# Moving y's products to the head of the next masked products, with lora between their halves

## The reference

```python
def rwkv7_scan(r, decay, k, v, kk, a):
    def step(S, inp):
        sa = -jnp.einsum('bhvk,bhk->bhv', S, kk_t)
        S = S * w_t[:, :, None, :] + sa[..., None] * b_t[:, :, None, :] + v_t[..., None] * k_t[:, :, None, :]
        y = jnp.einsum('bhvk,bhk->bhv', S, r_t)
        return S, y
...
mean = jnp.mean(y, axis=-1, keepdims=True)
var = jnp.mean(jnp.square(y - mean), axis=-1, keepdims=True)
y = ((y - mean) * lax.rsqrt(var + LNX_EPS)).reshape(B, T, RWKV_WIDTH) * lnx_gain + lnx_bias
```

## Time and profile before

| what | value |
|---|---|
| median of 3 runs | 1822.35 us (1821.75 to 1823.31) |
| the profiled execution | 1822.79 us, its span 1820.8 us |
| TensorE clock granted | 0.998 of full |
| busy: PE, DVE, ACT, POOL | 99%, 69%, 46%, 26% |
| chain that ended last | PE 95%, DVE 3%, ACT 1% |
| line 1404, share of that chain | 70% |

### The profile page before, as it was taken

One profiled execution on the slowest core, in us unless ns is written; L12 is line 12 of the kernel. 1 busy time (PEld: TensorE's weight loads), 2 busy tenths in 40 slices (PEclk: granted clock), 3 DMA queues, 4 the chain that ended last, 5 costly groups with the idle time before them and its releaser, 6 DMA issues.

```text
span 1820.8 us, 37389 instructions
## 1 busy us (share of the span) xinstructions
PE 1803.7 (99%) x14519; PEld 1479.8 (81%) x14519; DVE 1248.6 (69%) x2255; ACT 832.0 (46%) x1725; POOL 476.8 (26%) x1093
## 2 busy tenths in 40 slices
PE   9999999999999999999999999999999999999997
PEld 7778888888888888888888888888888788888886
DVE  5876777777767688667777777776778854345445
ACT  7544445454535355444453545353535553242335
POOL 0014233241505060142432415050606060100110
PEclk9999999999999999999999999999999999999999
DMA  8633333333333345433333333333323543466546
GB/s 302 198 92 91 92 97 86 97 92 91 98 92 99 84 108 166 114 86 92 96 87 96 92 96 95 91 100 83 106 78 107 166 138 103 130 202 202 167 126 231
DMA packets 200289, 217.09 MB, mean 119 GB/s; under 512 B 98864, under 2 KB 104112, under 8 KB 199472
## 3 DMA queue, kind: packets, MB, share of 16 engines
q1 hardware_dynamic: 190032, 197.19, 37.6%
q10 hardware_dynamic: 10080, 17.51, 3.4%
HBM read 192.61 MB, written 22.02 MB: 118 GB/s over the span
## 4 chain that ended last, share of the span: by engine, by line
PE 95%; DVE 3%; ACT 1%; issue 1%; DMA 0%; ACTq 0%; SPq 0%; DVEq 0%
PE psum L1404 70%; PE psum L1389 3%; PE psum L1679 3%; PE psum L1681 3%; PE psum L1680 3%; PE psum L1522 2%; PE psum L1462 2%; PE psum L1490 1%; PE psum L1671 1%; PE psum L1555 1%; PE psum L1635 1%; DVE w_lo L929 1%; PE psum L1642 1%; PE psum L1424 1%; PE psum L1623 1%
## 5 line engine op out<-in xcount | busy, mean ns | idle before, releaser
L1404 PE MATMUL psum<-x_hi,w_hi 128*128 128x512 f32 x1888 | 763.5, 404 | 2.5 <-DVE x_lo L938 2.2
L1404 PE MATMUL psum<-x_hi,w_lo 128*128 128x512 f32 x1888 | 738.5, 391 | 0.0
L1404 PE MATMUL psum<-x_lo,w_hi 128*128 128x512 f32 x1888 | 736.3, 390 | 0.0
L929 DVE TENSOR_TENSOR w_lo<-w_raw,w_hi 128x512 fp32r<-128x512 f32 x522 | 368.2, 707 | 393.2 <-ACT w_hi L665 362.6
L665 ACT ACTIVATE w_hi<-w_raw 128x512 fp32r<-128x512 f32 x522 | 326.1, 628 | 665.9 <-PE psum L1404 596.7
L1404 PEld LDWEIGHTS psum<-x_hi,w_hi 128*128 128x128 f32 x1888 | 355.2, 188 | 87.6 <-DVE w_lo L929 9.9
L1404 PEld LDWEIGHTS psum<-x_hi,w_lo 128*128 128x128 f32 x1888 | 354.6, 188 | 77.2
L611 POOL TENSOR_TENSOR sub_t<-sub_l,sub_io 128x60 f32<-128x60 f32 (+24 forms) x496 | 192.5, 388 | 850.1 <-DMA sub_l<-scratch_L 812.5
L1404 PEld LDWEIGHTS psum<-x_lo,w_hi 128*128 128x128 f32 x1888 | 355.7, 188 | 66.9 <-issue 0.5
L613 POOL TENSOR_TENSOR sub_io<-sub_io,sub_t 128x60 f32<-128x60 f32 (+24 forms) x496 | 207.1, 418 | 38.8
L1679 PE MATMUL psum<-w_hi,x_hi 128*128 128x512 f32 x256 | 100.3, 392 | 1.4 <-DVE w_lo L929 1.2
(11 more groups left out here) (276 smaller groups left out, 2092.8 us busy)
## 6 DMA issues: line engine op xcount, KB each, us to landing
w_raw<-in_w_in SPq DMA_DIRECT2D x348, 256.0 KB, 2.7
w_raw<-in_w_in ACTq DMA_DIRECT2D x60, 256.0 KB, 2.8
w_raw<-in_w_out SPq DMA_DIRECT2D x60, 256.0 KB, 2.7
w_raw<-in_w_rows SPq DMA_DIRECT2D x50, 256.0 KB, 2.8
stage<-in_w_rows SPq DMA_DIRECT2D x30, 256.0 KB, 2.8
sub_l<-scratch_L SPq DMA_DIRECT2D x16, 384.0 KB, 4.1
stage<-in_x_t SPq DMA_DIRECT2D x20, 256.0 KB, 4.2
stage<-scratch_MIX SPq DMA_DIRECT2D x19, 256.0 KB, 3.7
```

The lines of the kernel that those rows point to most:

```text
L929: nc.vector.tensor_tensor(w_lo[gq % SPLIT][:], w_raw[raw_of(gq)[0]][:], w_hi[gq % SPLIT][:].bitcast(F32), ALU.subtract).then_inc(w_ready, 1)
L1404: mm = nc.tensor.matmul(psum[:, bank_of(s)], wt[gq % SPLIT][:, cols], xx[:, c], start=(c == 0 and wt is w_hi and xx is x_hi), stop=(c == K ...
```

## The change

- On TensorE, y's products leave place 24. They become `outputs(i)` and stand at the head of place 25, in front of the next interval's `products(i + 1, 0)`; for intervals 6 and 15, which have no masked products there, they stand alone at the head of place 25.
- lora's products leave the place behind the masked products and stand between their two halves.
- On VectorE, the two adds of y go from place 24 to 25, behind `low` and the slices of x and in front of the masked copies. Centring goes from the end of place 24 to the end of 25. The sum of squares goes from 26 to 28, and the reciprocal and the scaling from 27 to 29.
- On ScalarE, the Square goes from 25 to 27 and the Sqrt from 27 to 29.

```diff
@@ ScalarE
-                    if at == 25:
+                    if at == 27:
                         act.wait_ge(y_centred, i + 1)
...
-                    if at == 27:
+                    if at == 29:
                         act.wait_ge(y_var, i + 1)
@@ VectorE
+                def read_y(i):
+                    dve.wait_ge(y_full, i + 1)
+                    dve.wait_ge(h_read, i + 1)
...
+                    dve.sem_inc(y_read, 1)
...
-                    if at == 24:
...
-                    if at == 26:
+                    if at == 28:
                         dve.wait_ge(y_squared, i + 1)
...
-                    if at == 27:
+                    if at == 29:
                         spread = [P, BH, HD]
                         dve.wait_ge(y_root, i + 1)
...
                     if pair:
                         slices(*pair)
                     for j, at in current(gq):
+                        if j >= 1 and at == 25:
+                            read_y(j - 1)
+                    for j, at in current(gq):
                         if j >= 1 and at == 1:
                             masked(j - 1, 0)
                             masked(j - 1, 1)
...
-                        if j >= 1 and at == 24:
+                        if j >= 1 and at == 25:
                             centre(j - 1)
@@ TensorE
+                def outputs(i):
+
+                    pe.wait_ge(gt_ready, i + 1)
...
+                    mm.then_inc(y_full, 1)
...
                 def recurrence(i, at):
                     if at == 1:
+                        if i not in (0, PAIRS - 1):
+                            outputs(i - 1)
                         products(i, 0)
+                        if i < INTERVALS - 1:
+                            lora_products(i + 1)
                         products(i, 1)
+                    if at == 25 and i in (PAIRS - 2, INTERVALS - 1):
+                        outputs(i)
```

More of the change, by code:

```diff
@@ L1206, in transition @@
                     dve.sem_inc(gt_ready, 1)
+                def read_y(i):
+                    dve.wait_ge(y_full, i + 1)
+                    dve.wait_ge(h_read, i + 1)
+                    for hh in range(2):
+                        ins = nc.vector.tensor_tensor(
+                            y[:, :, hh], psum[:, 4 + hh, 0:NB * HD].rearrange("p (b d) -> p b d", b=NB),
+                            hs[:, :, hh], ALU.add)
+                    then(ins)
+                    dve.sem_inc(y_read, 1)
                 def centre(i):
@@ L1408, in quarter, with lora_products @@
                             mm.then_inc(w_used, 1)
-                def channels(j, at):
[L1411 to L1425, removed]
+                def lora_products(j):
+                    h = j // PAIRS
+                    pe.wait_ge(up_landed[j % 2], 16 * (j // 2 + 1))
+                    pe.wait_ge(lora_ready, 2 * h + 2)
+                    pe.wait_ge(rooted, h + 1)
+                    pe.wait_ge(inv_ready, j)
+                    pe.wait_ge(bonus_read, j)
+                    if j >= 2:
+                        pe.wait_ge(mixa_ready, j - 1)
+                    if j >= 3:
+                        pe.wait_ge(yt_read, PAIRS - 1 if j == PAIRS else j - 2)
+                    for x in range(2):
+                        rows = slice(x * LORA, (x + 1) * LORA)
+                        nc.tensor.matmul(psum[:, 2 + x], lora_up[j % 2][rows, :], lora[rows, :],
+                                         start=True, stop=True).then_inc(lora_done, 1)
+                def channels(j, at):
+                    if j == 0 and at == 3:
+                        lora_products(j)
                     if at == 4 and j % PAIRS == 0:
@@ L1466, in products @@
                     mm.then_inc(a_full, 1)
+                def outputs(i):
+                    pe.wait_ge(gt_ready, i + 1)
+                    for b in range(NB):
+                        for c in range(2):
+                            for hh in range(2):
+                                rows = slice(hh * HD, (hh + 1) * HD)
+                                mm = nc.tensor.matmul(psum[vs_rows(c), 4 + hh, b * HD:(b + 1) * HD],
+                                                      gt[rows, b, c], states[rows, 2 * b + c],
+                                                      start=True, stop=True, skip_group_check=True)
+                    mm.then_inc(y_full, 1)
                 def turns(i):
@@ L1647, in recurrence @@
                         chain(i, 2 * (at - 21) + 1)
[L1648 to L1657, removed]
                     if at == 31:
```

## The result

| | before | changed kernel |
|---|---|---|
| median of 5 runs | 1822.4 us (1821.75 to 1823.44) | 1829.48 us (1827.26 to 1830.75) |
| ratio, 95% interval | | 1.0037 (1.0027 to 1.0048) |
| profiled execution | 1822.79 us | 1830.06 us |
| span, granted clock | 1820.8 us, 0.998 | 1828.1 us, 0.997 |
| busy PE, DVE, ACT, POOL | 99%, 69%, 46%, 26% | 99%, 69%, 46%, 26% |

What follows compares the result with a forecast made beforehand. PE's own list was taken as the bound. Regular heads -1.8, dead heat +0.6, break before interval 7 +0.8, interval 15 +2.0, last y +0.05: +1.7 on 1822.35 gives 1824.1 us, range 1820.8 to 1829.0.

Steps and rivals of the forecast that it cites:

- the bound: PE, busy for 99% of the span: the change gives only what it takes out of PE's own list, start to start.
- 0.76 saved at place 24: Regular interval on PE: without y the bonus follows the chain 0.13 us later instead of 0.89, so 0.76 us shorter.
- 0.63 spent at 25: Regular interval on PE: y runs 0.63 us to the first masked product, leaving a gain of 0.14 us per interval.
- lora free: PE, between the masked products' halves: lora adds nothing, it takes its 0.96 us wherever it stands.
- y_read: PE's second half of masked products waits for DVE's read of y: hidden by 0.2 us, by lora alone.
- A dead heat: Place 33: division ends so PE can go on at 231.79, PE wants its transposes at 231.78; 0.6 us over 13 intervals.
- the first rival: DVE falls behind p_norm at place 33: PE waits 0.5 us per interval, 1830 us; chance 0.24.
- interval 15: Its head: nothing gained at place 24, second half resumes 3.55 us later, old wait for masked copies goes; net +2.0 us.
- the break before interval 7: Place 24 still waits for DVE's read of a tile, y stands alone at place 25: +0.8 us, nothing back.
- ACT's fourth table load: Exp loaded again before the scores' Exp at place 31, 1.28 us, hidden by 0.3 us; as a rival 1836 us, chance 0.04.
- the late DVE: Same as the first rival: DVE late for p_norm, PE loses 13 times all beyond another 0.05 us; chance 0.24.
- The prediction's own signs of being wrong: PE's wait on the division at place 33 0.3 us or more per interval, or regular heads shorter by more than 0.3.

## Why the prediction was wrong

- **Right: the bound.** PE's own list, read from start to start, was the right ledger. 0.76 saved at place 24 (0.77), 0.63 spent at 25 (0.62), lora free (it even gave 0.02).
- **Right, with its size: y_read.** "Hidden by lora alone; without lora between, 0.7 us would be lost in each interval": 0.78 measured.
- **Wrong, the decisive step: "A dead heat … I put 0.05 us per interval".** It was 0.26 (0.20 of wait and 0.06 behind it), 3.4 us where 0.6 stood. The mechanism was right and was even the first rival; the term was mis-sized. The sum took 14 us of DVE instructions at the durations they had in the kernel before and put their end 0.01 us from the point where PE wants it. In the new order the same list is longer: from w_lo of place 28 to the end of the division the sum has 13.88 us (217.8 to 231.68), measured were 13.99 to 14.14 in 11 intervals and 14.44 to 14.45 in two. In interval 1 DVE ended 0.12 later than worked out and PE came 0.08 earlier. Errors of 0.1 us on either side have to be expected in such a sum, and they are not symmetric: coming early gives nothing, coming late costs in full, 13 times. A tie has to be priced at the spread of its terms, not at its mean. The two long intervals had a DVE pause of 0.50 us in place of the usual 0.15 (at 391.87 and 651.99), and it went through to PE (0.54 and 0.52 us at place 33); in the kernel before such a pause stood at 387.54, in slack. What makes these pauses no run here shows, but "the intervals repeat to some hundredths of a us" holds for PE's steps, not for DVE's pauses.
- **Wrong: place 36.** The prediction followed DVE's list only up to the first wait that PE has for it, and so put this term at nothing. The lateness doesn't end there; it meets the next consumer three quarters on, with 1.7 us.
- **Half right: interval 15.** The wait for y was right to 0.01 us, the release of the old wait for the masked copies too. What was missing is the clock: PE idle for 2.94 us, then 1.6 us lost at 1.2 GHz.
- **Right: the break before interval 7** (0.8 forecast, 0.9 measured), and that nothing is gained at place 24 there.
- **ACT's fourth table load** stayed hidden in the changed kernel, as worked out: ACT's work for the division ends at 229.73, where 229.8 was forecast, and DVE comes to it at 230.24. It is hidden by DVE's own lateness, though; with the sum of squares at 27, DVE waited for it. In interval 1 of the changed kernel:

```profile
226.47 1.28 ACT L753 ACT_TABLE_LOAD   x1
227.77 0.46 ACT L753 ACTIVATE score<-score,top 128x192 f32<-128x192 f32 x1
```

The Exp starts 0.02 us behind the load. The Trainium skill ("ScalarE: Activation LUTs", What ACT_TABLE_LOAD costs) puts a drain of about 1380 ns on top of each switch of table; this trace has no such time, neither behind the load nor in front of it (the w_hi before it started at 225.82 and ended at 226.45).

The range ended at 1829.0 because the late DVE was given 0.24 and its upper part left out. With the clock and place 36 missing, the sum would have reached that end only at 0.43 us per interval at place 33. The prediction's own signs of being wrong, 0.3 us or more of that wait and heads shorter by more than 0.3, did not come (0.26 and 0.16): they watched two terms, and 3.3 of the 5.6 us that the forecast lacked came from the two that it didn't have.

## What to carry to other kernels

A step moved out of an engine's pause into its busy stretch is paid by everyone behind it in that stretch: ask of each moved instruction not only who waits for it, but which pause it leaves and whose slack it takes, and follow the lateness past the first consumer. Where two engines meet at the same 0.1 us in an order that repeats, price the meeting at its spread times the repeats. And where a kernel's order has breaks, keep the old order there when the new one has nothing to gain: three special cases were worth more than the regular gain.

## What the runs showed of the hardware

- After PE waits of 2.92 to 2.94 us its granted clock went to half, already in the wait or up to 1.5 us into the work behind it, in all four traces that have such a wait (the changed kernel twice, the sum of squares at 27, lora behind), and cost 1.4 to 1.6 us in the two of the changed kernel. At the waits of 1.72 us (y's adds in front, one trace) and 1.35 us (the kernel before) it stayed at 1.00. No limit follows from this: near its start the kernel before is at 0.50 from 7.80 to 11.20 us, with waits of 0.97 and 1.28 us there, and of the ten runs of the changed kernel one, without a trace, took 1827.26 us at a mean clock of 0.999.
- From the end of a DVE instruction to the start of the matmul that waits for it, 0.11 to 0.12 us pass, and the matmul behind that one comes 0.05 to 0.1 us later than usual (0.16 in place of 0.11 at place 33, 0.33 in place of 0.23 at place 36). At place 33 of interval 1 none of it shows as idle time.
- Going from 64x64 to 64x128 tiles cost y's products 0.14 us against the 0.48 that 32 records take by themselves (rows 3), as much as going to 128x128. The Trainium skill ("TensorEngine Tiling (Array Packing)", Key Properties) says that a change of tiling mode drains TensorE; the trace agrees, with 0.14 to 0.15 us each time.
